# A two-layer MoE trunk on one core: how layer 1's experts get their token columns, where an odd expert's first products stand, and how the first attention weights are loaded

## What is computed

```python
D_MODEL = 1024; N_EXPERTS = 16; TOP_K = 2; D_EXPERT = 512
...
    gates = jnp.sum(jax.nn.one_hot(idx, N_EXPERTS, dtype=F32) * w[..., None], axis=1)
    def expert(y, p):
        wg, wu, wd, ge = p
        a = jax.nn.silu(t @ wg) * (t @ wu) * ge[:, None].astype(t.dtype)
        return y + a @ wd, None
...
        x = x + g1 * mix
        h = rmsnorm(x, norm_ffn_g[i]) * (1 + sc2) + sh2
        x = x + g2 * group_moe(h, w_router, router_bias, moe_w_gate[i], moe_w_up[i], moe_w_down[i])
```

## Time and profile before

| | |
|---|---|
| runs | 1439.5, 1441.8, 1443.28 us; median 1441.8 |
| profiled execution | 1440.93 us, its span 1439.0 us |
| PE busy | 1354.5 us, 94% of the span |
| DVE, ACT, POOL busy | 517.8, 282.2, 47.2 us |
| moved by DMA | 344.83 MB, mean 240 GB/s |
| gate/up products (L1089, L1090), both layers | about 228 us of PE time with both halves at once |
| gather products (L986) | 106.4 us for 384 products |

### The profile page before, as it was taken

How to read it: one execution, slowest core, us unless ns; L and a number is a source line. 1 busy time by engine, 2 the same in 40 slices (tenths; PEclk the granted TensorE clock), 3 DMA queues, 4 the chain that set the end, 5 groups by cost and what they waited for, 6 DMA issues and landing times.

```text
span 1439.0 us, 17852 instructions
## 1 busy us (share of the span) xinstructions
PE 1354.5 (94%) x6816; PEld 768.3 (53%) x6816; DVE 517.8 (36%) x1376; ACT 282.2 (20%) x580; POOL 47.2 (3%) x63
## 2 busy tenths in 40 slices
PE   5899999997998999889999999999998998899997
PEld 2456556555444444447667567576565544444434
DVE  3145355625111111554464653744513311111123
ACT  3143344411010111231120221212111100001013
POOL 1001200000000000100000000100100000000010
PEclk9999999998999999999999999999999899999998
DMA  9967686926999999912323423224534799579891
GB/s 363 322 244 231 224 279 237 380 95 238 392 396 350 398 395 378 388 64 94 117 82 117 146 88 110 95 89 139 182 118 174 254 398 387 190 258 398 324 399 52
DMA packets 162742, 344.83 MB, mean 240 GB/s; under 512 B 5929, under 2 KB 23554, under 8 KB 162626
## 3 DMA queue, kind: packets, MB, share of 16 engines
q1 hardware_dynamic: 150320, 319.19, 60.4%
q10 hardware_dynamic: 9362, 14.37, 2.7%
q0 software_dynamic: 2944, 9.65, 2.5%
HBM read 324.96 MB, written 18.22 MB: 238 GB/s over the span
## 4 chain that ended last, share of the span: by engine, by line
PE 85%; DMA 6%; DVE 4%; ACT 2%; SPq 2%; issue 1%; DVEq 0%; ACTq 0%
PE psum L1089 14%; PE psum L771 11%; PE psum L786 10%; PE psum L808 9%; PE psum L1120 7%; PE psum L986 7%; PE psum L1206 5%; PE psum L937 3%; PE psum L1198 3%; DMA ring<-in_moe_w_up 3%; PE psum L673 2%; PE psum L1031 2%; DMA ring<-in_da_w_qkv 2%; SPq L569 1%; PE psum L1060 1%
## 5 line engine op out<-in xcount | busy, mean ns | idle before, releaser
L771 PE MATMUL psum<-hT,ring 128*128 128x384 f32 x512 | 173.5, 498 | 8.8 <-DMA ring<-in_da_w_qkv 5.9
L1089 PE MATMUL psum<-ring,work 128*64 128x512 f32 x384 | 170.1, 593 | 2.6 <-DMA ring<-in_moe_w_up 2.6
L1090 PE MATMUL psum<-ring,work 128*64 128x512 f32 x384 | 170.2, 594 | 0.0
L771 PEld LDWEIGHTS psum<-hT,ring 128*128 128x128 f32 x512 | 99.0, 195 | 77.4 <-issue 8.3
L808 PE MATMUL psum<-ring,hT 128*128 128x512 f32 x288 | 125.9, 593 | 0.0
L986 PE MATMUL psum<-work 128*128 128x128 f32 x768 | 106.4, 292 | 5.5 <-issue 3.5
L1089 PEld LDWEIGHTS psum<-ring,work 128*64 128x64 f32 x384 | 51.8, 137 | 111.2 <-issue 111.0
L986 PEld LDWEIGHTS psum<-work 128*128 128x128 f32 x768 | 95.0, 200 | 28.2 <-issue 24.0
L1120 PE MATMUL psum<-ring,work 128*64 128x512 f32 x192 | 89.9, 612 | 1.3 <-issue 1.2
L1975 DVE COPY work<-psum 128x512 f32<-128x512 f32 x32 | 22.1, 692 | 191.2 <-PE psum L1121 191.2
L1121 PE MATMUL psum<-ring,work 128*64 128x512 f32 x192 | 90.0, 613 | 0.0
(11 more groups left out here) (338 smaller groups left out, 1810.0 us busy)
## 6 DMA issues: line engine op xcount, KB each, us to landing
ring<-in_w_ada SPq DMA_DIRECT2D x24, 2048.0 KB, 12.4
ring<-in_moe_w_gate SPq DMA_DIRECT2D x24, 2048.0 KB, 13.0
ring<-in_moe_w_up SPq DMA_DIRECT2D x24, 2048.0 KB, 17.4
ring<-in_moe_w_down SPq DMA_DIRECT2D x24, 2048.0 KB, 17.9
ring<-in_da_w_qkv SPq DMA_DIRECT2D x6, 2048.0 KB, 14.8
sq<-in_moe_w_gate SPq DMA_DIRECT2D x8, 1536.0 KB, 12.3
hT<-in_moe_w_up SPq DMA_DIRECT2D x8, 1536.0 KB, 15.0
work<-in_moe_w_down SPq DMA_DIRECT2D x24, 512.0 KB, 11.3
```

Source lines behind the costliest of these rows:

```text
L771: last = mm(b[:, 0:TOK], w[:, kt, col:col + P], hT[:, kt, :], start=kt == 0, stop=kt == KT - 1)
L1089: mm(psum[0:BLK, x, :], xk, wg[kt], start=kt == 0, stop=kt == KT - 1)
L1090: last = mm(psum[BLK:P, x, :], xk, wu[kt], start=kt == 0, stop=kt == KT - 1)
```

## The change

Four parts.

1. Layer 1 only: the 24 gather products of pairs 1 to 7 go. ACT stores `htok` to HBM (`token_rows`, 1.5 MB in two DMAs, semaphore `kept`) before the experts. For each pair PE multiplies `sel` with a column of token numbers (`list_tokens`: three products of one column), DVE casts the 128 numbers to `ids` (`token_list`), POOL fetches these 128 rows of 4 KB with an indirect DMA into `xrow` (`row_loads`), PE turns them with eight transposes (`turn_rows`) into the same two PSUM banks, and ACT copies them to `xs`. `xrow` takes the place of the second buffer of `xs`. Pair 0 is gathered as before. `select` and `list_tokens` run two pairs ahead, the fetch one: it is issued when the pair before has been turned.
2. The gate/up products of an odd expert for kt 0 to 2 move into the even expert before it (`gate_up`, `pipelined`): kt 0 and 1 between the even expert's gate/up and its transposes, kt 2 between these and its down products. In layer 1 for all odd experts, in layer 0 for expert 15 alone. List, first six turns and last two turns stand at the same two places of the odd experts, in layer 1 alone.
3. `side_work` of expert 15 moves from kt 1, 3, 5, 7 to kt 4, 5, 6, 7, in both layers.
4. The first query and key units are loaded in halves of 1 MB: query half 0, key half 0, tables, query half 1, key half 1. Head 0 needs half 0 alone; heads 1 to 3 follow, and the whole unit is waited for at head 2.

```diff
-    plan = {(e, 2 * i + 1): pair(e - 1, i) for e in range(LAST + 1, NE) for i in range(4)}
+    plan = {(e, AHEAD + 1 + i): pair(e - 1, i) for e in range(LAST + 1, NE) for i in range(4)}
...
-                        sp.dma_start(att_tab, att_d).then_inc(in_att, 16)
+                        for half in range(2):
+                            for kind in "qk":
+                                here = slice(256 * half, 256 * half + 256)
+                                to, src = source((kind, 0))[0]
+                                sp.dma_start(to[:, :, here], src[:, :, here]).then_inc(slot_full[slot_of[(kind, 0)]] if half else in_first[kind], 16)
+                            if half == 0:
+                                sp.dma_start(att_tab, att_d).then_inc(in_att, 16)
+                    elif name != ("k", 0):
+                        load(name)
...
-                if i == 0:
+                if h == 0:
+                    pe.wait_ge(in_first[kind], 16)
+                elif h == 2 or i == 0:
...
+                def list_tokens(q):
+
+                    pe.wait_ge(m["sel"], q + 1)
+                    if q > 1:
+                        pe.wait_ge(m["listed"], q - 1)
+                    chosen = sel_second if q == 1 else sel
+                    for t in range(TT):
+                        last = mm(psum[:, 4, 0:1], chosen[:, t].rearrange("p x s -> p (x s)"),
+                                  table(base_sb, base_at, "token")[:, t:t + 1], start=t == 0, stop=t == TT - 1)
+                    last.then_inc(m["ids"], 1)
+
+                def turn_rows(q, kts):
+
+                    pe.wait_ge(m["rows"], 16 * q)
+                    pe.wait_ge(m["xs"], 2 * q)
+                    for kt in kts:
+                        last = tr(psum[:, 2 + kt // 4, P * (kt % 4):P * (kt % 4) + P], xrow[:, P * kt:P * kt + P], ident)
+                        if kt % 4 == 3:
+                            last.then_inc(m["gathered"], 1)
+
                 pe.wait_ge(m["sel"], 1)
-                for half in range(2):
-                    gather(half, range(4 * half, 4 * half + 4)).then_inc(m["gathered"], 1)
+                gather(0, range(4)).then_inc(m["gathered"], 1)
                 emptied(pe, ("rank", l))
+                if l:
+                    list_tokens(1)
+                gather(1, range(4, KT)).then_inc(m["gathered"], 1)
                 pe.wait_ge(m["routed"], 1)
+                def gate_up(e, kts):
+
+                    wg, wu = unit(e, 0), unit(e, 1)
+                    q, x = divmod(e, 2)
+                    for kt in kts:
+                        if x == 0 and kt % 4 == 0:
+                            pe.wait_ge(m["xs"], q * 2 + kt // 4 + 1)
+                        xk = xs[:, 0 if l else q % 2, kt, BLK * x:BLK * x + BLK]
+                        mm(psum[0:BLK, x, :], xk, wg[kt], start=kt == 0, stop=kt == KT - 1)
+                        last = mm(psum[BLK:P, x, :], xk, wu[kt], start=kt == 0, stop=kt == KT - 1)
+                        if kt == KT - 1:
+                            last.then_inc(m["gu"], 1)
+                        side_work((e, kt))
+                    return wg, wu
+
...
-                            wg, wu = unit(e, 0), unit(e, 1)
...
+                            pipelined = lambda n: n % 2 == 1 and (l == 1 or n == NE - 1)
+                            gate_up(e, range(AHEAD if pipelined(e) else 0, KT // 2))
+                            hint = pe.mark_branch_hint_location()
+                            wg, wu = gate_up(e, range(KT // 2, KT))
                             overflow(e, wg, wu, hint)
                             more = q + 1 < NE // 2
-                            if more:
+                            if pipelined(e + 1):
+                                gate_up(e + 1, range(AHEAD - 1))
+                            if more and l == 0:
                                 pe.wait_ge(m["sel"], q + 2)
                                 pe.wait_ge(m["xs"], q * 2 + x + 1)
                                 gather(x, range(4 * x, 4 * x + 3))
+                            if more and l and x:
+                                if q + 2 < NE // 2:
+                                    list_tokens(q + 2)
+                                turn_rows(q + 1, range(6))
...
-                            if more:
+                            if pipelined(e + 1):
+                                gate_up(e + 1, range(AHEAD - 1, AHEAD))
+                            if more and l == 0:
                                 gather(x, (4 * x + 3,)).then_inc(m["gathered"], 1)
+                            if more and l and x:
+                                turn_rows(q + 1, range(6, KT))
...
+                if l:
+                    for half in range(2):
+                        emptied(act, ("htok", l, TT * half + TT - 1))
+                        act.dma_start(token_rows_d.rearrange("(t p) d -> p t d", p=P)[:, :, 512 * half:512 * half + 512],
+                                      htok[:, :, 512 * half:512 * half + 512]).then_inc(m["kept"], 16)
...
-                            if q + 1 < NE // 2:
+                            if q + 1 < NE // 2 and l == 0:
                                 take_xs(q + 1, 1 - par, x)
+                            if q + 1 < NE // 2 and l and x:
+                                take_xs(q + 1, 0, 0)
+                                take_xs(q + 1, 0, 1)
...
+                def token_list(q):
+
+                    dve.wait_ge(m["ids"], q)
+                    V.tensor_copy(ids[:, q:q + 1], psum[:, 4, 0:1]).then_inc(m["listed"], 1)
+
                 select(0)
+                if l:
+                    select(1)
...
-                        if q + 1 < NE // 2:
+                        if l == 0 and q + 1 < NE // 2:
                             dve.wait_ge(m["gathered"], q * 2 + 2)
                             select(q + 1)
+                        if l and q + 2 < NE // 2:
+                            if q == 0:
+                                dve.wait_ge(m["gathered"], 2)
+                            select(q + 2)
...
+                            if l and x and q + 2 < NE // 2:
+                                token_list(q + 2)
...
+            def row_loads():
+
+                m = M[1]
+                pool.wait_ge(m["kept"], 32)
+                for q in range(1, NE // 2):
+                    pool.wait_ge(m["listed"], q)
+                    if q > 1:
+                        pool.wait_ge(m["gathered"], 2 * q)
+                    pool.indirect_dma_start(out=xrow, out_offset=None, in_=token_rows_d,
+                                            in_offset=bass.IndirectOffsetOnAxis(ap=ids[:, q:q + 1], axis=0)).then_inc(m["rows"], 16)
```

34 lines of the change are left out of this document (17 added, 17 removed).

## The result

The changed kernel takes 1465.07 us (median of 4 runs, 1463.52 to 1470.61) where the kernel before takes 1442.12. The ratio is 1.0158, 95% interval 1.0136 to 1.0181: slower by some 23 us. I had forecast 1446, with 1436 to 1454 as the range.

The account below looks back on a forecast made before the run. Expert stages were taken as limited by both PE and the DMA of weights. Terms 0.5 + 6.2 − 2.4 = +4.3 on the profiled 1440.93 gave 1445.2, as a median 1446 us; range 1436 to 1454.

Parts of the forecast that it names:

- That moved instructions cost nothing: PE's program: no term for where its instructions lie; layer 0's experts 0 to 13 stood at 0.
- Layer 0's end: Layer 0, experts 13 to 15: PE waits 7.6 us for expert 15's up weights; loses 6.2 us (4.5 to 7.5).
- The term 4.5 + 1.7: Behind expert 15's up landing: expert 14's transposes and down products 4.5 us, slow clock 1.7; 6.2 us in each layer.
- the DMA chain: Layer 1's weight queue: expert 7's transposes 15.3 us earlier, expert 15's up weights landing at 1384, 8.6 us earlier.
- The 8 us for sharing with the picks: Layer 1's end: six picks share DMA with the last weights, delaying expert 15's up weights 8 us (4 to 10).
- 28 us of saved PE work: Layer 1, seven pairs without gather: 28 us if PE alone counted, which DMA would prevent.
- The start: First query and key loads in halves: +0.5 us (−2.0 to +3), value products gaining at most 2.0 us.
- The 0 to 1.1 us that I allowed for shorter segments: Halved first query and key loads: segments of 1 KB instead of 2 cost 0 to 1.1 us.
- (b): Layer 1: row fetches served behind queued weights arrive after their 22 us; +8 us, 1454; chance 0.12.
- (d): Layer 1: the clock falls at each turn of a pair; +4 us, 1450; chance 0.04.
- (c): Layer 1: PE alone counts and weights don't bind; 1420 to 1425 us; chance 0.12.
- (a): Layer 1's end: picks too late to share or fewer queue holes, up 15 by 1376; 1438 or 1436; chance 0.15.

Follow-up runs that it names:

- after_pad62: The changed kernel with 62 semaphore increments that nobody waits for in front of PE's program; 1459.9 us, ratio 1.0113.
- pad2: The kernel before with 2 increments of an unused semaphore in front of PE's program; 1448.9 us, ratio 1.0049.
- after_late_pad: The changed kernel with 62 idle increments before PE's program and both layers' picks held until expert 15's up weights landed; 1447.8 us, ratio 1.0041.
- pad64: The kernel before with 64 increments of an unused semaphore in front of PE's program; 1442.3 us, ratio 1.0005.
- only_halves: The kernel before with only the first query and key weights loaded in halves; 1450.1 us, ratio 1.0049.
- best variant: The changed kernel with ahead products only for layer 1's experts 3 to 11, whole query/key loads, 64 idle PE increments, picks held; 1430.75 us, ratio 0.9922.
- only_fetch: The kernel before with only layer 1's gather replaced by fetched and turned rows; 1467.7 us, ratio 1.0177.

## Why the prediction was wrong, step by step

The forecast was +4.3 on the profiled execution; +24.4 came. By the milestones of the table, with after_pad62 beside it, where the stall at expert 3 is gone:

| step | forecast | measured | after_pad62 |
|---|---|---|---|
| start, to layer 0's expert 0 | +0.5 | +2.1 | +1.4 |
| layer 0, experts 0 to 13 | 0 | +4.9 | −2.1 |
| layer 0's end, 13 to 15 | +6.2 | +10.4 | +11.8 |
| from there to layer 1's expert 0 | 0 | +2.1 | +1.4 |
| layer 1, to expert 15 | −2.4 | 23.0 − 19.5 = +3.5 | +6.1 |
| behind it | 0 | +1.4 | +0.2 |
| sum | +4.3 | +24.4 | +18.8 |

Three steps failed: moved code was put at nothing, layer 0's landing was taken as unchanged, and layer 1's last landing was put 8.6 us earlier. The first is 5 us of the miss; the other two stay in after_pad62.

**That moved instructions cost nothing.** I costed the changed code at the stages it serves and took the rest of the program as fixed. The stall at expert 3, shown by pad2 and gone in after_pad62, is 3.28 us and the slow clock behind it, together +4.9 by expert 13; the medians give 1465.1 − 1459.9 = 5.2. No view of the kernel before shows it as a threat. It does show its kind: the waits by "issue" there, the longest 2.50 us, which I had passed over.

**Layer 0's end: right mechanism, mis-sized twice.** PE stood as forecast, behind expert 14's products and ended by `in_moe_w_up`, 10.14 us instead of 7.6. The term 4.5 + 1.7 counts from the landing to expert 15's transposes. From landing to transpose it was 593.6 − 580.3 = 13.3 us before and 611.0 − 589.6 = 21.4 after, 8.1 more; half of the 5.9 us at 0.50 is 3.0, not 1.7, so the clock is most of that miss. Counted from PE's start on expert 15 this price is 6.9 to 7.3 us in both layers of after_pad62 and after_late_pad, so the term was short by some 0.9 us; the other microsecond of the changed kernel is not there in that place. The other 2.3 us are the landing itself, 20.7 us behind its issue where it had 18.4. I took that landing as unchanged. It is a tie: in the kernel before the picks start at 574.32, in the same moment in which the gate weights land (561.39 issued, 574.3 landed), and up follows 6.0 us later. In after_pad62 they start 1.8 us ahead of the gate weights (572.83, 574.6), and up follows 9.4 behind; with the picks held it is 5.4. A start of the picks 1 to 2 us earlier costs 3 us. In every variant with other expert code the gate weights land later behind their issue, 13.7 to 14.5 us, against 12.4 to 12.9 in the kernel before, pad2, pad64 and only_halves, and behind 62 or 64 increments the picks start 0.4 to 0.7 us sooner; why, is not shown.

**Layer 1: the DMA chain held, its input was short.** Counted from the stage's own start, expert 7's transpose came 13.0 us earlier (forecast 15.3), expert 13's up weights 8.6 us earlier (forecast 11.3, 1352.5 − 1341.2), expert 15's 5.0 us earlier (8.6): the shortfall is 2.3 us at the first step, 2.7 at the second and 3.6 at the last. In after_pad62 it is larger: expert 7 came 9.3 us earlier and expert 15's up weights 0.8 (1404.3, less 12.4 for the start, against 1392.6), so of the 8.6 us forecast almost nothing was left. Part of that is the stall of 2.64 us within the first turns; the rest is not taken apart. The 8 us for sharing with the picks was good: holding them brought the landing from 1404.3 to 1391.8, of which 5.3 is that the whole kernel ran earlier, 7.2 us of sharing. The price behind the landing was 8.5 us in place of 6.2; 4.2 us of PE's work at 0.50 are 2.1 of it, and PE stood 3.32 us ahead of expert 15's transposes where the kernel before stood 2.29. In after_pad62 it was 6.9. 28 us of saved PE work was rightly not expected to count.

**The start:** the value products start at 53.41 after 5.51 us of idle, and take 22.28 us where they took 20.76, +0.5 behind them as forecast. The first query products, forecast at 35.1, start at 36.91, later than before, without harm, since the value weights bind. The 0 to 1.1 us that I allowed for shorter segments no run shows by itself: the value weights land 1.0 us later than forecast here, and not later in only_halves (52.14). The 1.6 us that come after that are not taken apart; to layer 0's expert 0 the variants differ from the kernel before by −0.3 to +2.8 us, the largest in pad64, which has nothing of the change.

```profile
53.41 2.08 PE L823 MATMUL psum<-ring,hT 128*128 128x512 f32 x2 [5.51 <-DMA ring<-in_da_w_qkv]
```

**The rivals.** (b) did not happen. POOL's issues of the first two row fetches in the changed kernel, and the slowest landing of the seven:

```profile
1147.15 0.98 POOL L2242 DMA_INDIRECT work<-token_rows,work  x1 [99.82 <-DMA token_rows<-work]
1167.43 0.94 POOL L2242 DMA_INDIRECT work<-token_rows,work  x1 [19.30 <-PE psum L1105]
...
work<-token_rows,work POOLq DMA_INDIRECT x1, 9.8
```

With 8.0 to 9.8 us to land and some 22 to have, PE never waited for rows. The Trainium skill's fit (DMA: Bandwidth & Descriptors, "Anatomy of one DMA") gave an estimated 3.2 us and would have been two and a half to three times too low here. (d) did not happen: the granted clock of the changed kernel is 1.00 in every 25 us from 1150 to 1350. (c) was reached for a while, PE being 18.5 us early at expert 12 in the best variant, and ended at the full DMA engines as the text said. (a), picks that don't share, did not happen: they do share, and taking them out of the way is what pays.

What I should have given is a slower outcome with 1454 to 1466 in the range: two copies of a price of 6.2 us with its upper bounds, the picks' tie in layer 0, and an allowance of 5 to 10 us for the place of the code.

What stays open: by which rule PE's instruction blocks are fetched early or not, and so which place is a good one before it is measured; how much of the stalls by "issue" at the down products (3.7 us in seven of them in layer 1, the longest 1.1) is of the same kind; and where the rest of layer 1's shortfall comes from.

## What to carry to other kernels

Before crediting an edit with a few microseconds, measure it in two places: 2 to 64 idle instructions in front of the engine's program moved variants of this kernel by up to 11 us, about as much as the edits themselves. When an in-order engine is given work ahead, ask what it stands in front of if its data is late, and when the DMA engines are full at that point, look which other transfer may wait: holding six small gathers behind one load, in both layers, was worth 10 to 14 us, where the faster engine alone was worth nothing, and the holding alone too. Ties between a load and a transfer from another queue are worth a line of their own in a forecast, since a start 1 to 2 us earlier decides them.

## What the hardware showed that I had not expected

- Two instructions in front of PE's program cost 6.7 us (1442.3 to 1448.9; by the ratio's interval 2 to 12), 64 cost nothing. The stall is 3.3 to 3.6 us, with a 16 KB instruction block on DMA queue 8 that comes only then. In seven of the eight traces that have it the clock is at 0.5 for 3.4 to 6.8 us more; in only_fetch it stays at 1.00.
- In and behind a wait of 10 us or more the granted clock stayed at 0.5 for 10 to 17 us in all, and 3 to 6 us of PE's work fell into that.
- Short gathers from GpSimd (6 picks, 3.1 MB) delay a hardware load of 2 MB that is already queued from 5.3 to 13.3 us behind its predecessor if they start 5 us ahead of that predecessor's landing, to 8.7 to 9.6 if 1.4 to 2.0 us ahead, and to no more than 6.6 if they start with it.
